# Sparse attention loop: eight score buffers, four score banks, one bank for the sums, and two heads' small probabilities in one copy

## The chip, the cores and the metric

The kernel runs on one core of a Trainium2 chip, in one launch. The metric is the device time of a run in microseconds (us), as the median of several runs; lower is better. PE is the TensorE (matmuls and transposes), DVE the VectorE, ACT the ScalarE, POOL the GpSimd engine, SP the SyncE. All numbers are float32.

## The reference, cut to what matters

Two decoder layers over 512 tokens of width 1024. Layer 0 is an mLSTM and differential attention with an FFN, layer 1 is native sparse attention with an FFN. The change touches only one part of layer 1: the two of its three attention branches that are computed as masked dense attention (the gathered top-6 blocks, and the window of 256 keys), with 16 heads of 64 features in 4 key/value groups:

```python
s_s = jnp.einsum('bqghd,bgqmd->bghqm', qr, k_g).astype(jnp.float32) * scale
p_s = jax.nn.softmax(jnp.where(mask_s, s_s, NEG_INF), axis=-1)
o_s = jnp.einsum('bghqm,bgqmd->bqghd', p_s.astype(v_g.dtype), v_g)
```

and the same for the window with its keys. Both outputs are multiplied by a sigmoid gate of each token and head, and added to the output of the compressed branch.

## The kernel before, in words

The engines run separate instruction streams, written out by hand, and meet only by semaphores. In layer 1 the projections end, the compressed branch is computed, and then comes **the loop** that the change is in. Behind it the summed rows are turned back to features (L1066, L1435, L2061) and the output projection begins (L551 to L553).

The loop's unit of work is a *set* `n`: one block of 128 queries, one branch, one head. There are 128 sets: four query blocks, two branches, sixteen heads. `SET_ORDER` (L171) puts them in this order of query block and branch, each for all sixteen heads: sets 0 to 47 have three key tiles of 128 keys, sets 48 to 63 four, sets 64 to 95 two, sets 96 to 127 one. Eight sets of one kind are a *batch* `b`, 16 in all. What is done for a set:

- *scores* (`set_scores`, L1000, PE): one matmul, 64 features deep, 128 queries by 128 to 512 keys, into bank `n % 2` of the PSUM tensor `aux`.
- *max* (`set_max`, L2013, DVE): one instruction scales, adds the mask, writes the negated scores to the score buffer `sr[n % 4]` and gives the row's negated maximum.
- *exp* (L1419, ACT): the exponential in place in the same buffer, with the row's sum.
- *turn* (`set_turn`, L1009, PE): one transpose per key tile, into bank `2 + n % 2` of `aux`.
- *take* (`take_probs`, L475 on ACT, L477 on DVE): the turned probabilities copied to SBUF, every third set by ACT, the others by DVE.

And for a batch:

- *values* (`set_values`, L1023, PE): one pair of matmuls for each key tile, 512 columns each, one key tile per step; the sums of the batch add up in a PSUM bank called `OB`.
- the sums copied by ACT (L1431, `branch_sums`, which frees `OB`), turned by PE (`sums_turn`, L1033) into a bank called `OT`, multiplied with the coefficients (the reciprocal sum times the gate, L2021 and L2025) by DVE (`batch_out`, L2036, which frees `OT`), and added to the output rows by POOL (L2222). `OB` and `OT` have two banks each, used in turns (L155).

All engines go through the loop in *steps* `n = 0, 2, 4, ...`, two sets at a time. A step of PE is: scores of sets `n` and `n+1`; turns of sets `n-4` and `n-3`; `sums_turn` if a batch has its turn; then at most one key tile of values for a batch. Values of batch `b` begin at step `8b + 12`. A step of DVE: two maxes; one of the 16 instructions of the top-6 selection and its masks (`select_step`, one each in steps 2 to 32); its takes of `n-4`, `n-3`; coefficients; `batch_out`. A step of ACT: two exps; its takes; the copy of sums.

The waits that order the loop before the change: the scores of step `n` wait until both maxes of step `n-2` are done (L995), since there are two score banks. The max of set `n` waits until set `n-4` is turned (L2003), since there are four score buffers, and that turn stands in PE's stream behind the scores of the same step. The turn of set `n` waits for the take of set `n-2` (L1007), since there are two turn banks. Everything that an engine's stream has behind a waiting instruction waits too.

The banks before: `aux` 0 and 1 scores, `aux` 2 and 3 turns, the four banks of `abank` for `OB` and `OT`. No weight is loaded during the loop; the output projection's first weights are already split when it begins.

Of the kernel before, what the change touches and what calls it, by code (L numbers as in the profile page):

```python
# [11 lines left out]
P = 128  # L12
D = 1024
T = 512
# [202 lines left out]
def on_act(n):  # L217

    return n % 3 == 0


def taken_before(n):

    return sum(on_act(k) == on_act(n) for k in range(n + 1))
# [11 lines left out]
def trunk(nc, A, consts, out):  # L236
    with ExitStack() as ctx:
# [95 lines left out]
        sr = [row(f"score{s}", 36 + s if s < 3 else 6, 1) for s in range(4)]  # L333
# [17 lines left out]

        TR = abank[2][:, 0:P]
# [112 lines left out]
        def take_probs(eng, n):  # L465

            i, win, h = set_of(n)
            w = set_tiles(i, win) * P
            eng.wait_ge(S("s_turned"), n + 1)
            b = n // 8  # L470
            if b >= 2:
                eng.wait_ge(S("s_sum"), b - 1)
            dst = eT[b % 2][:, n % 8 * T:n % 8 * T + w]
            if on_act(n):
                eng.activation(dst, aux[:, 2 + n % 2, 0:w], ACT.Copy).then_inc(S("probs_by_act"), 1)  # L475
            else:
                eng.tensor_copy(dst, aux[:, 2 + n % 2, 0:w]).then_inc(S("probs_by_dve"), 1)  # L477

        def wait_probs(eng, n):
            eng.wait_ge(S("probs_by_act" if on_act(n) else "probs_by_dve"), taken_before(n))  # L480
# [67 lines left out]
        def _(pe):  # L548
# [453 lines left out]

            def set_turn(n):
                i, win, h = set_of(n)
                pe.wait_ge(S("s_exp"), n + 1)
                if n >= 2:
                    wait_probs(pe, n - 2)  # L1007
                for s in range(set_tiles(i, win)):
                    mm = pe.transpose(aux[:, 2 + n % 2, col(s)], sr[n % 4][:, col(s)], ident)  # L1009
                mm.then_inc(S("s_turned"), 1)  # L1010

            def set_values(b, s):
                i, win, h = set_of(8 * b)
                keys, tiles = set_keys(i, win), set_tiles(i, win)
                if s == 0:
                    wait_probs(pe, 8 * b + 7)
                    wait_probs(pe, 8 * b + 6)
                    wait_probs(pe, 8 * b + 5)
# [19 lines left out]
            for n in range(0, sums_turned_at(NSETS // 8 - 1) + 4, 2):  # L1038
# [10 lines left out]
                for b in batches_at(sums_turned_at, n - 2):  # L1049
# [6 lines left out]
            for q in range(8):  # L1056
# [4 lines left out]
                else:  # L1061
                    wait_probs(pe, NSETS - 1)
                    wait_probs(pe, NSETS - 2)
# [12 lines left out]
        def _(act):  # L1076
# [333 lines left out]
            for n in range(0, sums_turned_at(NSETS // 8 - 1) + 2, 2):  # L1410
                for m in (n, n + 1):
                    if m >= NSETS:
                        break
# [5 lines left out]
                    act.activation(sr[m % 4][:, 0:w], sr[m % 4][:, 0:w], ACT.Exp, scale=-1.0,  # L1419
                                   bias=nmx[:, m % 16:m % 16 + 1], accum_out=rsum[:, m % 16:m % 16 + 1])\  # L1420
                       .then_inc(S("s_exp"), 1)
                for m in (n - 4, n - 3):
                    if 0 <= m < NSETS and on_act(m):
                        if m == 0:
                            act.wait_ge(S("c_sum"), 2 * TT)
                        take_probs(act, m)
                for b in batches_at(sums_turned_at, n):
                    if b >= 2:
                        act.wait_ge(S("sums_turned"), b - 1)
                    act.wait_ge(S("s_sum"), b + 1)  # L1430
                    act.activation(osum[b % 2], ps(("OB", b))[:, :], ACT.Copy).then_inc(bank_free(("OB", b)), 1)  # L1431
# [29 lines left out]
        def _(dve):  # L1461
# [537 lines left out]
            def set_max(n):  # L1999
                i, win, h = set_of(n)  # L2000
                w = set_tiles(i, win) * P
                if n >= 4:
                    dve.wait_ge(S("s_turned"), n - 3)  # L2003
# [9 lines left out]
                dve.tensor_tensor_reduce(sr[n % 4][:, 0:w], aux[:, n % 2, 0:w], mask, -(HD ** -0.5), BIG,  # L2013
                                         ALU.add, ALU.min, nmx[:, n % 16:n % 16 + 1]).then_inc(S("s_max"), 1)

            def batch_coef(b):
# [6 lines left out]
                if b >= 2:  # L2023
                    wait_taken(dve, ("OT", b - 2))
# [17 lines left out]
            for n in range(0, sums_turned_at(NSETS // 8 - 1) + 4, 2):  # L2042
# [8 lines left out]
                for m in (n - 4, n - 3):  # L2051
                    if 0 <= m < NSETS and not on_act(m):
                        take_probs(dve, m)
# [205 lines left out]
```

## Time and profile before

| what | us |
|---|---|
| median of three runs | 1431.55 |
| the three runs | 1424.27, 1431.55, 1432.41 |
| the profiled execution, whole | 1428.94 |
| its span, first to last instruction | 1427.1 |
| the loop within it, first scores to last turned sums | 823.0 to about 992 |
| PE busy in the span | 1355.2 (95%) |
| DVE, ACT, POOL busy in the span | 711.1, 551.5, 279.2 |

The profile is of one execution, and the times inside it add up to its own span; around the span lie 1.84 us. The median of the other runs is 2.6 us above that execution. "Busy" counts an instruction from its first to its last moment; matmuls overlap one another at their ends, so that PE is shown busy where it only drains. Where a text speaks of the *spacing* of instructions, it means from start to start, which has no such overlap.

### The profile page before, as it was taken

Reading aid. Unit: us, or ns where it says so; the run is one execution under the profiler, and the core shown is the slowest. Engines: PE = TensorE matmul, PEld = TensorE weight load, DVE = VectorE, ACT = ScalarE, POOL = GpSimd, SP = SyncE. Lnnn points to the kernel's source line nnn. Section 1 sums busy time; section 2 is a strip of 40 time slices with the busy share of each in tenths; the row PEclk is TensorE's granted clock in tenths of the full one; section 3 lists DMA queues with packets and bytes.
Section 4 is the critical chain, followed back from the end, with each engine's and each line's share of the span. In section 5 each row is a group of like instructions: output and inputs, shape, how many; then the busy total and the mean of one; then the engine's idle time right before and its main releaser. Section 6 shows DMA issues by size and latency. Waiting matters only on the chain.

```text
span 1427.1 us, 18120 instructions
## 1 busy us (share of the span) xinstructions
PE 1355.2 (95%) x6431; PEld 1059.5 (74%) x6431; DVE 711.1 (50%) x1279; ACT 551.5 (39%) x1009; POOL 279.2 (20%) x268
## 2 busy tenths in 40 slices
PE   7999989999999999999999988987989999999998
PEld 6777667888888888888777744444778888888887
DVE  4459865544434333333898677665344343433222
ACT  4335655433333322222453345565243333332222
POOL 2057352221111110011355001112111111111010
PEclk9999999999999999999999999998899999999999
DMA  7322221333333334322343200000123333343321
GB/s 219 89 59 60 59 60 45 89 89 103 88 103 90 101 108 118 88 83 74 103 118 107 62 16 1 1 1 1 59 74 103 103 88 103 89 119 101 101 61 60
DMA packets 203946, 114.12 MB, mean 80 GB/s; under 512 B 5713, under 2 KB 200529, under 8 KB 203761
## 3 DMA queue, kind: packets, MB, share of 16 engines
q1 hardware_dynamic: 203264, 112.97, 27.0%
q0 software_dynamic: 416, 0.35, 0.3%
q8 instruction: 33, 0.54, 0.2%
q14 instruction: 25, 0.20, 0.0%
q10 hardware_dynamic: 208, 0.06, 0.0%
HBM read 111.27 MB, written 2.10 MB: 79 GB/s over the span
## 4 chain that ended last, share of the span: by engine, by line
PE 81%; DVE 8%; ACT 5%; issue 3%; POOL 2%; DMA 0%; DVEq 0%; POOLq 0%; SPq 0%; ACTq 0%
PE acc L551 23%; PE acc L553 22%; PE acc L552 22%; PE aux L1009 3%; PE aux L1000 2%; PE acc L1023 2%; DVE w_low L459 2%; ACT score L1419 1%; ACT w_high L440 1%; DVE cmp_in_low L1685 1%; PE acc L1033 1%; PE acc L960 0%; PE aux L678 0%; PE aux L668 0%; DVE work L1532 0%
## 5 line engine op out<-in xcount | busy, mean ns | idle before, releaser
L459 DVE TENSOR_TENSOR w_low<-raw,w_high 128x1024 fp32r<-128x1024 f32 (+1 forms) x187 | 250.7, 1341 | 531.5 <-ACT w_high L440 531.2
L551 PE MATMUL acc<-y_high,w_high 128*128 128x512 f32 x1056 | 421.2, 399 | 12.0 <-DVE w_low L451 6.4
L552 PE MATMUL acc<-y_low,w_high 128*128 128x512 f32 x1056 | 414.8, 393 | 0.0
L553 PE MATMUL acc<-y_high,w_low 128*128 128x512 f32 x1056 | 414.7, 393 | 0.0
L440 ACT ACTIVATE w_high<-raw 128x1024 fp32r<-128x1024 f32 (+1 forms) x187 | 206.8, 1106 | 345.1 <-PE acc L553 336.1
L551 PEld LDWEIGHTS acc<-y_high,w_high 128*128 128x128 f32 x1056 | 200.2, 190 | 57.5 <-DVE w_low L451 7.9
L553 PEld LDWEIGHTS acc<-y_high,w_low 128*128 128x128 f32 x1056 | 199.9, 189 | 43.2
L552 PEld LDWEIGHTS acc<-y_low,w_high 128*128 128x128 f32 x1056 | 200.3, 190 | 41.8 <-issue 0.7
L551 PE MATMUL acc<-ffn_high,w_high 128*128 128x512 f32 (+1 forms) x374 | 141.0, 377 | 0.0
L552 PE MATMUL acc<-ffn_low,w_high 128*128 128x512 f32 (+1 forms) x374 | 140.8, 377 | 0.0
L553 PE MATMUL acc<-ffn_high,w_low 128*128 128x512 f32 (+1 forms) x374 | 140.8, 377 | 0.0
L2139 POOL TENSOR_TENSOR work<-work,work 128x512 f32<-128x512 f32 x44 | 57.0, 1295 | 417.6 <-DVE work L1488 417.6
L1419 ACT ACTIVATE score<-score,neg_max 128x384 f32<-128x384 f32 (+3 forms) x128 | 69.1, 541 | 64.7 <-DVE neg_max L2013 64.6
L2125 POOL TENSOR_TENSOR work<-work,work 128x512 f32<-128x512 f32 x31 | 41.8, 1347 | 228.1 <-ACT work L1086 227.7
L1488 DVE TENSOR_TENSOR work<-acc,rinv 128x512 f32<-128x512 f32 x107 | 73.2, 684 | 24.6 <-PE acc L553 17.1
L1267 ACT ACTIVATE ffn_high<-work 128x512 f32 (+1 forms) x44 | 27.8, 633 | 148.5 <-POOL work L2139 148.5
L551 PEld LDWEIGHTS acc<-ffn_high,w_high 128*128 128x128 f32 x374 | 70.4, 188 | 13.0
L553 PEld LDWEIGHTS acc<-ffn_high,w_low 128*128 128x128 f32 x374 | 70.4, 188 | 12.8
L552 PEld LDWEIGHTS acc<-ffn_low,w_high 128*128 128x128 f32 x374 | 70.4, 188 | 12.8
L2013 DVE CUSTOM_DVE_ANT_0 score<-aux,shape_constants 128x384 f32<-128x384 f32 (+2 forms) x112 | 45.8, 441 | 40.4 <-PE aux L1009 39.4
L1009 PEld LDWEIGHTS aux<-shape_constants,score 128*128 128x128 f32 x304 | 32.6, 140 | 35.8 <-ACT score L1419 29.9
L1262 ACT ACTIVATE work<-work 128x512 f32<-128x512 f32 x44 | 27.8, 633 | 80.3 <-DVE work L1488 80.3
(282 smaller groups left out, 1597.5 us busy)
## 6 DMA issues: line engine op xcount, KB each, us to landing
raw<-in_l_w_in_dram SPq DMA_DIRECT2D x44, 512.0 KB, 3.7
raw<-in_l_w_gate_dram SPq DMA_DIRECT2D x44, 512.0 KB, 3.7
raw<-in_l_w_up_dram SPq DMA_DIRECT2D x44, 512.0 KB, 3.7
raw<-in_l_w_down_dram SPq DMA_DIRECT2D x32, 704.0 KB, 4.5
raw<-in_l_w_out_dram SPq DMA_DIRECT2D x16, 512.0 KB, 3.5
x_rows<-in_x_dram SPq DMA_DIRECT2D x4, 512.0 KB, 5.6
raw<-in_l_cmp_w_k_dram SPq DMA_DIRECT2D x4, 512.0 KB, 3.6
raw<-in_l_cmp_w_v_dram SPq DMA_DIRECT2D x4, 512.0 KB, 3.8
```

The source lines that it names most:

```text
L440: act.activation(dst, src, ACT.Copy).then_inc(S("split_high"), 1)
L459: dve.tensor_tensor(dst, src, high.bitcast(F32), ALU.subtract).then_inc(S("split_low"), 1)
L551: pe.matmul(o, ah, bh, start=first, stop=False)
L552: pe.matmul(o, ah, bl, start=False, stop=False)
L553: return pe.matmul(o, al, bh, start=False, stop=last)
L1000: pe.matmul(aux[:, n % 2, 0:keys.stop - keys.start], qrot[a, q], k, start=True, stop=True).then_inc(S("s_scores"), 1)
L1009: mm = pe.transpose(aux[:, 2 + n % 2, col(s)], sr[n % 4][:, col(s)], ident)
L1419: act.activation(sr[m % 4][:, 0:w], sr[m % 4][:, 0:w], ACT.Exp, scale=-1.0, bias=nmx[:, m % 16:m % 16 + 1], accum_out=rsum[:, m % 16:m % 1 ...
L1488: return dve.tensor_tensor(dst, ps(tile)[lo:hi, cols], rinv[lo:hi, cols], ALU.mult)
L2013: dve.tensor_tensor_reduce(sr[n % 4][:, 0:w], aux[:, n % 2, 0:w], mask, -(HD ** -0.5), BIG, ALU.add, ALU.min, nmx[:, n % 16:n % 16 + 1]).t ...
L2125: pool.tensor_tensor(tmp[0][:, 0:T], tmp[0][:, 0:T], tmp[1 + m % 2][:, 0:T], ALU.add)\
L2139: pool.tensor_tensor(up, tmp[2 * (t % 2)][:, 0:T], up, ALU.mult).then_inc(S("ffn_prod"), 1)
```

## The change

It rewrites who may use which buffer in the loop, and the order of a few steps; each matmul, transpose, max and exponential stays.

1. Score buffers: eight instead of four (`sr`), in rows of SBUF that are free by then. The max of set `n` waits for the turn of set `n-8`.
2. Score banks: four instead of two (`SCORE`): `aux` 0 and 1, `abank` 2 and 3. The scores of step `n` wait for the maxes of step `n-4`. The scores of sets 2 and 3, whose banks held the compressed branch's last tiles, wait until those were read (`OC` 6 and 7).
3. Sums: `OB` has only bank 0, `OT` only bank 1. `sums_turn` comes one step earlier in PE's stream (in the step in which ACT copies the sums), and ACT's copy stands before the step's exps instead of after its takes.
4. Takes: sets of one or two key tiles are turned two at a time into one bank (the second set behind the first), and copied by one instruction of twice the width; that is sets 64 to 127. Of all takes, counted one after another, every third is ACT's. Turn banks of these pairs alternate by pair.
5. The wait for `OT` in `batch_coef` stands before the reciprocal.

```diff
         elif kind in ("OB", "OT"):
-            b = k % 2 + 2 * (kind == "OT")
+            b = int(kind == "OT")
...
-def on_act(n):
-
-    return n % 3 == 0
...
+TAKES = []
+for _n in range(0, NSETS, 2):
+    TAKES += [(_n, 2)] if set_tiles(*set_of(_n)[0:2]) <= 2 else [(_n, 1), (_n + 1, 1)]
+TAKE_OF = {first + k: t for t, (first, count) in enumerate(TAKES) for k in range(count)}
...
+def on_act(t):
+
+    return t % 3 == 0
...
+def turn_bank(n):
+
+    return 2 + (n // 2 if TAKES[TAKE_OF[n]][1] == 2 else n) % 2
...
+def turn_column(n):
+
+    return n % 2 * set_tiles(*set_of(n)[0:2]) * P if TAKES[TAKE_OF[n]][1] == 2 else 0
...
+def taken_first(n):
+
+    return [max(TAKE_OF[m] for m in range(n) if turn_bank(m) == turn_bank(n) and TAKE_OF[m] < TAKE_OF[n])] if n >= 2 else []
...
-        sr = [row(f"score{s}", 36 + s if s < 3 else 6, 1) for s in range(4)]
+        sr = [row(f"score{s}", r, 1) for s, r in enumerate((36, 37, 38, 6, 41, 7, 42, 43))]
...
+        SCORE = [aux[:, 0, :], aux[:, 1, :], abank[2][:, :], abank[3][:, :]]
...
-            dst = eT[b % 2][:, n % 8 * T:n % 8 * T + w]
-            if on_act(n):
-                eng.activation(dst, aux[:, 2 + n % 2, 0:w], ACT.Copy).then_inc(S("probs_by_act"), 1)
+            dst = eT[b % 2].rearrange("p (h t) -> p h t", t=T)[:, n % 8:n % 8 + count, 0:w]
+            src = aux[:, turn_bank(n), 0:count * w].rearrange("p (h t) -> p h t", h=count)
+            if on_act(t):
+                eng.activation(dst, src, ACT.Copy).then_inc(S("probs_by_act"), 1)
...
-                if n >= 2:
-                    pe.wait_ge(S("s_max"), n // 2 * 2)
+                if n >= 4:
+                    pe.wait_ge(S("s_max"), n // 2 * 2 - 2)
+                elif n >= 2:
+                    for k in (6, 7):
+                        wait_taken(pe, ("OC", k))
...
-                pe.matmul(aux[:, n % 2, 0:keys.stop - keys.start], qrot[a, q], k,
+                pe.matmul(SCORE[n % 4][:, 0:keys.stop - keys.start], qrot[a, q], k,
...
-                if n >= 2:
-                    wait_probs(pe, n - 2)
+                for t in taken_first(n):
+                    wait_probs(pe, t)
+                c = turn_column(n)
                 for s in range(set_tiles(i, win)):
-                    mm = pe.transpose(aux[:, 2 + n % 2, col(s)], sr[n % 4][:, col(s)], ident)
+                    mm = pe.transpose(aux[:, turn_bank(n), c + s * P:c + (s + 1) * P], sr[n % 8][:, col(s)], ident)
...
-                for b in batches_at(sums_turned_at, n - 2):
+                for b in batches_at(sums_turned_at, n):
                     sums_turn(b)
...
+                for b in batches_at(sums_turned_at, n):
+                    if b >= 2:
+                        act.wait_ge(S("sums_turned"), b - 1)
+                    act.wait_ge(S("s_sum"), b + 1)
+                    act.activation(osum[b % 2], ps(("OB", b))[:, :], ACT.Copy).then_inc(bank_free(("OB", b)), 1)
+                for m in range(n, min(n + 2, NSETS)):
...
-                if n >= 4:
-                    dve.wait_ge(S("s_turned"), n - 3)
+                if n >= 8:
+                    dve.wait_ge(S("s_turned"), n - 7)
...
                 dve.wait_ge(S("s_exp"), 8 * b + 8)
+                if b >= 2:
+                    wait_taken(dve, ("OT", b - 2))
                 dve.reciprocal(coef[:, c:c + 8], rsum[:, c:c + 8]).then_inc(S("s_recip"), 1)
                 dve.wait_ge(S("s_recip"), b + 1)
-                if b >= 2:
-                    wait_taken(dve, ("OT", b - 2))
```

## Rows read from the trace of the kernel before

**Rows 1.** The page: the chain that ended last, share of the span by engine.

```profile
PE 81%; DVE 8%; ACT 5%; issue 3%; POOL 2%; DMA 0%; DVEq 0%; POOLq 0%; SPq 0%; ACTq 0%
```

**Rows 2.** Windows of the loop's five stretches: us, busy us (instructions) of PE, PEld, DVE, ACT, POOL, then the granted clock.

```profile
830.93:841.51 10.58, 7.06 (x41) 3.74 (x41) 7.40 (x26) 5.98 (x19) 0.00 (x0) 1.00 0.00 0
841.51:893.80 52.29, 46.98 (x253) 21.26 (x253) 38.32 (x123) 30.07 (x91) 5.10 (x4) 1.00 0.00 1
893.80:919.90 26.10, 23.54 (x126) 10.88 (x125) 17.59 (x49) 15.57 (x41) 2.54 (x2) 1.00 0.01 1
919.90:957.89 37.99, 35.27 (x202) 16.47 (x201) 24.90 (x99) 23.07 (x81) 5.09 (x4) 1.00 0.01 1
957.89:986.11 28.22, 22.36 (x138) 11.73 (x136) 17.17 (x97) 18.16 (x80) 5.08 (x4) 1.00 0.00 1
```

**Rows 3.** Source view of L1000 (scores): what ended PE's idle time before it, us and times.

```profile
  DVE neg_max L2013: 63.2, 80
```

**Rows 4.** Timeline, a step without values: start us, us, engine, line, operation, idle before.

```profile
836.45 0.92 PE L1000 MATMUL aux<-k_win_dup,q_rot 64*128 64x384 f32 x4 [0.81 <-DVE neg_max L2013]
...
837.30 1.00 PE L1009 MATMUL aux<-shape_constants,score 128*128 128x128 f32 x6
...
837.88 0.56 DVE L2013 CUSTOM_DVE_ANT_0 score<-aux,shape_constants 128x384 f32<-128x384 f32 x1 [0.90 <-PE aux L1009]
...
838.98 0.92 PE L1000 MATMUL aux<-k_win_dup,q_rot 64*128 64x384 f32 x4 [0.68 <-DVE neg_max L2013]
```

**Rows 5.** Timeline of PE, a step of three tiles with values, and the next scores.

```profile
844.62 0.92 PE L1000 MATMUL aux<-k_win_dup,q_rot 64*128 64x384 f32 x4
...
845.47 0.88 PE L1009 MATMUL aux<-shape_constants,score 128*128 128x128 f32 x6
...
846.27 1.08 PE L1023 MATMUL acc<-probs_T,v_sel_win 128*64 128x512 f32 x4
...
847.28 0.92 PE L1000 MATMUL aux<-k_win_dup,q_rot 64*128 64x384 f32 x4
```

**Rows 6.** Timeline of PE, the sums turned and the values after them.

```profile
854.51 0.66 PE L1033 MATMUL acc<-shape_constants,branch_sums 128*128 128x128 f32 x4
...
855.10 1.08 PE L1023 MATMUL acc<-probs_T,v_sel_win 128*64 128x512 f32 x4
```

**Rows 7.** Timeline of DVE ahead of the loop's second step.

```profile
828.20 1.49 DVE L1991 TENSOR_TENSOR o_rows<-acc,gates 128x512 f32<-128x512 f32 x2 [1.24 <-PE acc L960]
```

**Rows 8.** Timeline of PE, a step of four tiles.

```profile
906.59 1.13 PE L1000 MATMUL aux<-k_sel_dup,q_rot 64*128 64x512 f32 x4
...
907.65 1.09 PE L1009 MATMUL aux<-shape_constants,score 128*128 128x128 f32 x8
...
908.67 1.08 PE L1023 MATMUL acc<-probs_T,v_sel_win 128*64 128x512 f32 x4
```

**Rows 9.** Timeline of PE, a step of two tiles.

```profile
930.45 0.70 PE L1000 MATMUL aux<-k_win_dup,q_rot 64*128 64x256 f32 x4
...
931.08 0.66 PE L1009 MATMUL aux<-shape_constants,score 128*128 128x128 f32 x4
...
931.67 1.08 PE L1023 MATMUL acc<-probs_T,v_sel_win 128*64 128x512 f32 x4
```

**Rows 10.** Timeline of PE, one tile: scores and turns.

```profile
971.03 0.49 PE L1000 MATMUL aux<-k_win_dup,q_rot 64*128 64x128 f32 x4
...
971.46 0.44 PE L1009 MATMUL aux<-shape_constants,score 128*128 128x128 f32 x2
```

**Rows 11.** Timeline of DVE: a copy of 512 columns, and two of 256.

```profile
925.00 0.69 DVE L477 COPY probs_T<-aux 128x512 f32<-128x512 f32 x1
...
927.36 0.75 DVE L477 COPY probs_T<-aux 128x256 f32<-128x256 f32 x2
```

**Rows 12.** Windows where the loop drains and behind it; columns as in rows 2.

```profile
988.00:990.00 2.00, 1.24 (x5) 0.20 (x4) 1.92 (x4) 0.27 (x1) 1.27 (x1) 0.80 0.00 0
...
991.95:1003.27 11.32, 7.95 (x35) 6.03 (x34) 6.23 (x9) 4.79 (x8) 1.26 (x1) 0.50 0.01 1
```

More of the change, by code:

```diff
@@ L214, in batches_at, with taken_before @@
     return [b for b in range(NSETS // 8) if at(b) == n]
-def on_act(n):
-    return n % 3 == 0
-def taken_before(n):
-    return sum(on_act(k) == on_act(n) for k in range(n + 1))
+TAKES = []
[4 more added lines that the diff above has]
+    return t % 3 == 0
+def taken_before(t):
+    return sum(on_act(k) == on_act(t) for k in range(t + 1))
+def turn_bank(n):
[4 more added lines that the diff above has]
+    return [max(TAKE_OF[m] for m in range(n) if turn_bank(m) == turn_bank(n) and TAKE_OF[m] < TAKE_OF[n])] if n >= 2 else []
 def gain_at(n, m, it=0):
@@ L463, in cmp_view, with take_probs @@
             return kvd[v].rearrange("p (g t) -> p g t", t=T)[:, :, 2 * c:2 * c + 16 * (NCMP - 1) + 1:16]
[L465 to L469, printed above, removed]
+        def take_probs(eng, t):
+            n, count = TAKES[t]
+            w = set_tiles(*set_of(n)[0:2]) * P
+            eng.wait_ge(S("s_turned"), n + count)
             b = n // 8
@@ L472, in take_probs, with wait_probs @@
                 eng.wait_ge(S("s_sum"), b - 1)
[L473 to L480 removed]
+            dst = eT[b % 2].rearrange("p (h t) -> p h t", t=T)[:, n % 8:n % 8 + count, 0:w]
+            src = aux[:, turn_bank(n), 0:count * w].rearrange("p (h t) -> p h t", h=count)
+            if on_act(t):
+                eng.activation(dst, src, ACT.Copy).then_inc(S("probs_by_act"), 1)
+            else:
+                eng.tensor_copy(dst, src).then_inc(S("probs_by_dve"), 1)
+        def wait_probs(eng, t):
+            eng.wait_ge(S("probs_by_act" if on_act(t) else "probs_by_dve"), taken_before(t))
         block = ctx.enter_context(nc.Block())
@@ L1015, in set_values @@
                 if s == 0:
-                    wait_probs(pe, 8 * b + 7)
-                    wait_probs(pe, 8 * b + 6)
-                    wait_probs(pe, 8 * b + 5)
+                    for t in range(TAKE_OF[8 * b + 7] - 2, TAKE_OF[8 * b + 7] + 1):
+                        wait_probs(pe, t)
                     wait_bank(pe, ("OB", b))
@@ L1037, in _ @@
             pe.wait_ge(S("rope_done"), 60)
-            for n in range(0, sums_turned_at(NSETS // 8 - 1) + 4, 2):
+            for n in range(0, sums_turned_at(NSETS // 8 - 1) + 2, 2):
                 if n < NSETS:
@@ L1061, in _ @@
                 else:
-                    wait_probs(pe, NSETS - 1)
-                    wait_probs(pe, NSETS - 2)
+                    wait_probs(pe, len(TAKES) - 1)
+                    wait_probs(pe, len(TAKES) - 2)
                 for m in range(4):
@@ L1418, in _ @@
                         act.wait_ge(S("s_coef"), m // 8 - 1)
-                    act.activation(sr[m % 4][:, 0:w], sr[m % 4][:, 0:w], ACT.Exp, scale=-1.0,
+                    act.activation(sr[m % 8][:, 0:w], sr[m % 8][:, 0:w], ACT.Exp, scale=-1.0,
                                    bias=nmx[:, m % 16:m % 16 + 1], accum_out=rsum[:, m % 16:m % 16 + 1])\
                        .then_inc(S("s_exp"), 1)
-                for m in (n - 4, n - 3):
-                    if 0 <= m < NSETS and on_act(m):
-                        if m == 0:
+                for t, (first, _count) in enumerate(TAKES):
+                    if first in (n - 4, n - 3) and on_act(t):
+                        if t == 0:
                             act.wait_ge(S("c_sum"), 2 * TT)
-                        take_probs(act, m)
-                for b in batches_at(sums_turned_at, n):
-                    if b >= 2:
-                        act.wait_ge(S("sums_turned"), b - 1)
-                    act.wait_ge(S("s_sum"), b + 1)
-                    act.activation(osum[b % 2], ps(("OB", b))[:, :], ACT.Copy).then_inc(bank_free(("OB", b)), 1)
+                        take_probs(act, t)
             for q in range(8):
@@ L2050, in _ @@
                     select_step(n // 2 - 1)
-                for m in (n - 4, n - 3):
-                    if 0 <= m < NSETS and not on_act(m):
-                        take_probs(dve, m)
+                for t, (first, _count) in enumerate(TAKES):
+                    if first in (n - 4, n - 3) and not on_act(t):
+                        take_probs(dve, t)
                 if n >= 10 and n % 8 == 2 and n < NSETS + 10:
```

6 lines of the change are left out of this document (1 added, 5 removed).

## The prediction

> **What bounds the kernel now.** I read the page's chain first [rows 1]: 81% of the span is on PE, almost all in the big projections, which the change leaves alone. So the question is one stretch of 170 us. I cut it where the kind of scores changes, at the first scores of steps 4, 12, 48, 64 and 96, up to the end of step 126, and read the windows of the five parts [rows 2]: A (steps 4 to 10, no values yet) 10.58 us, B (12 to 46, three tiles) 52.29, C (48 to 62, four tiles) 26.10, D (64 to 94, two tiles) 37.99, E (96 to 126, one tile) 28.22; in all 155.2 us for 62 steps. In none is an engine full: PE shows 135.2 us busy with overlaps counted twice, DVE 95.4, ACT 92.9. Three engines short of full, and the source view of the scores names what PE waits for: DVE's max, 63.2 us over 80 records [rows 3] (weight loads and matmuls are counted apart, so about half of it is wall time). That is the two-bank ring.
>
> The timeline shows the ring turning [rows 4]. Scores start at 836.45, the turns at 837.30, the first max only at 837.88, because it waits for the turn of set `n-4`, 1.43 us after the scores began. Two maxes take 1.10 us to 838.98, where the next scores start at once. The step lasts 2.53 us, although PE issues only 0.85 + 0.80 us of work in it. Where values fill the gap, it is the other way round [rows 5]: 844.62 to 847.28 is 2.66 us, put together without a hole from scores 0.85, turns 0.80, values 1.01. There PE is the bound already, and nothing can be gained in such a step. The gain lies in the steps with little PE work, and in the unevenness between steps.
>
> **Step by step: the floor of PE.** Spacings from the rows: two scores cost 0.85 us (three tiles) [rows 5], 1.06 (four) [rows 8], 0.63 (two) [rows 9], 0.43 (one) [rows 10]; turns of two sets 0.80, 1.02, 0.59 and, of one tile, at most 0.44 with their end, at least the half of that without it: I take 0.35; 0.45 for two tiles where no values follow, between 0.35 and 0.59. A key tile of values is 1.01 (V), sums turned 0.59 (U) [rows 5, 6]. The number of V and U in each part follows from `values_at` and the new place of `sums_turn`:
>
> A: 4 x (0.85 + 0.80) = 6.6. B: 18 x 1.65, 14 V, 4 U: 29.7 + 14.1 + 2.4 = 46.2. C: 8 x 1.06, turns 2 x 0.80 + 6 x 1.02, 6 V, 2 U: 8.5 + 7.7 + 6.1 + 1.2 = 23.5. D: 16 x 0.63, turns 2 x 1.02 + 10 x 0.59 + 4 x 0.45, 12 V, 4 U: 10.1 + 9.7 + 12.1 + 2.4 = 34.3. E: 16 x 0.43, turns 2 x 0.45 + 14 x 0.35, 5 V, 5 U: 6.9 + 5.8 + 5.1 + 3.0 = 20.8. Together 131.4, against 155.2: at most 23.8 us can go.
>
> **What the other engines leave of it, part by part.** Four score banks and eight buffers (edits 1 and 2) remove both links of the ring: scores need the maxes of two steps back, and the max no longer waits for a turn. What is late next is the turn's wait for the take of the step before. For three tiles, counted from the scores' start: 0.6 to the first result, 1.1 for two maxes [rows 4], about 0.4 for a selection step, two takes of about 0.5 each (between 0.75 for two of 256 columns and 0.69 for one of 512 [rows 11]): 3.1. The next turns come one step plus 0.85 later, so this binds only steps under 2.25 us. V steps (2.66) and U steps (2.24) clear it; the steps of A (1.65) don't.
> - A: DVE's own work is 7.40/4 = 1.85 per step [rows 2]; with the wait above about 2.1. I take 8.4, gain 2.2; bounds 6.6 and 10.58. In it is a late start: scores of step 2 now wait for DVE's last reads of the compressed branch, which end at 828.20 + 1.49 = 829.69 [rows 7]. The max of that step followed these reads on DVE anyway, and now comes at most 0.6 later; the next steps catch up, as scores may run ahead.
> - B: DVE 38.32/18 = 2.13 per step, PE's mean 2.57. DVE's coefficients and `batch_out` fall into the two steps behind a U step and put a max back by half a microsecond once a batch. I add 1.0 to 46.2: 47.2, gain 5.1; bounds 46.2 and 50.5.
> - C: DVE 2.20, ACT 1.95 per step against PE's 2.94: 23.7, gain 2.4.
> - D: DVE 1.56, ACT 1.44 against 2.14. A pair of takes by one instruction costs 0.69 where two cost 0.75 [rows 11], and turn banks now last two steps instead of one, so no turn waits. 34.9, gain 3.1; bounds 34.3 and 37.
> - E: the three engines lie close: PE 1.30 per step, ACT 18.16/16 = 1.14, DVE 1.07. In-order engines so near each other can't all be full; V and U steps (1.79, 1.37) alternate with steps of 0.78, in which ACT's 1.14 counts. Two steps of 1.14, one of 1.79 and one of 1.37 are 5.4 a batch, four of them 21.8; with DVE's coefficients and sums in the short steps I take 23.8, gain 4.4; bounds 20.8 and 27.
>
> Sum: 2.2 + 5.1 + 2.4 + 3.1 + 4.4 = 17.2 us.
>
> Edit 3 (one bank for the sums) I cost at nothing. `OB` must be copied by ACT (about 0.6 for 512 columns, a bank of the size of the 0.69 of DVE's copy [rows 11]) before the next batch's first V; between the last V and that one lie scores and turns of at least one step, 2.08 for four tiles [rows 8], where the next V follows closest. ACT's copy is queued ahead of two exps, but the first of these waits for a max that ends 1.1 after the scores' start. `OT` has eight sets' time to be read. `sums_turn` a step earlier falls, for three tiles, into the step that has no values, which evens PE out. If this cover were gone, the price is in the third rival. Edit 5 moves a wait on DVE's own earlier work: nothing. The tail behind step 126, and the row turns with their two engines behind them (11.32 us [rows 12]), stay. SP's and POOL's streams are untouched; no weight moves in the loop.
>
> A rule that speaks against edit 3: the Trainium skill, "Perfetto Trace Analysis", section "Optimizing Tensor Performance", says that independent groups of matmuls should rotate through different PSUM banks, so that the evacuation of one lies beside the next one's matmuls. The change takes this rotation from the sums and gives it to the scores. By the rule the sums' copy would be exposed; by the trace other matmuls fill that time, and the sum above stands. No run here shows it yet.
>
> The profiled execution would become 1428.94 - 17.2 = 1411.7. The median lies 2.6 above it; splitting this, I say 1413.0.
>
> **The rivals.**
> 1. Near the floor: gain 22 to 27. For it: B, C and D are PE-bound by my own numbers, and the clock falls to half (0.50 of 2.4, which is 1.2 GHz) only where the loop drains [rows 12]; a denser E might hold it. If the 11.32 us behind the loop ran at full clock, PE's 7.95 would halve, of which at most 3 are on its path. Against: E. Time 1428.94 - 24 + 1 = 1406.
> 2. The takes replace the ring: two turn banks remain, and if DVE reaches its takes some 0.3 us later than I have it, each step of A, B and C pays that, 30 x 0.3 = 9. Gain 8, time 1421 to 1423. For it: DVE shows 2.13 busy in a 2.9 us step already. Against: 0.4 us of room in the V steps.
> 3. Slower: the single `OB` bank, with ACT's copy ahead of the exps. By my count ACT ends a step's take about 2.9 after the scores' start, 0.25 after the end of a V (2.66), and then copies until 0.9 after it; the next exps could begin at 1.1. If ACT comes over 0.5 behind the V instead, copy and exps queue up, PE's `sums_turn` and the first V of the next batch wait for the copy, and the turns for the exps: copy 0.6 and two exps 1.3 (ACT's 1.67 per step [rows 2] less its takes), 1.9 on the path, once a batch, 16 x 1.9 = 30, less the 17 gained. Time about 1442. Against: scores and turns lie between the V and `sums_turn`, and two steps between an exp and its turn.
> 4. The limits are elsewhere and nothing moves: gain under 4, about 1430. Against: rows 4 show the wait itself.
>
> **How the numbers follow.** Forecast 0.56 (gain 12 to 22, or 1407 to 1419), rival 1 0.12, rival 2 0.22, rival 3 0.04, rival 4 0.06. The range reaches over the forecast into rivals 1 and 2: 1404 to 1423. A change of 1%, 14.3 us, is what a measurement of this kernel can tell from none. Faster by more than that, under 1417.2: all of rival 1 and most of the forecast, 0.12 + 0.56 less a part at its slow end, plus a little of rival 2's fast end, and the 2.6 us between profile and median mostly on my side: 0.70. Within 1%: 0.26. Slower: 0.04.
>
> **What would show it.** Right: a step without values lasts 1.7 to 2.2 us; PE's idle time before scores falls from 63.2 to under 10, and what is left moves to the turns, released by ACT's exps or the takes; V steps of three tiles stay at 2.66; A to E together last about 138; the takes of sets 64 to 127 are 32 instructions where they were 64. Wrong: PE idle ahead of the values or of L1033 with ACT's `branch_sums` as releaser (rival 3), or turns that wait for L477 in most steps of B (rival 2), or a granted clock below 1.00 inside the loop.

## The result, and the profile after

The changed kernel takes 1413.36 us (median of four runs, 1411.44 to 1416.21), the kernel before, with a fourth run beside it, 1428.32. The ratio is 0.9886, with a 95% interval of 0.9858 to 0.9914: 1.1% faster. Forecast were 1413.0 us. The span of the profiled execution fell from 1427.1 to 1411.6 us, by 15.5.

The page of the changed kernel, the chain by engine (as rows 1):

```profile
PE 83%; DVE 8%; ACT 4%; issue 3%; POOL 2%; DMA 0%; DVEq 0%; POOLq 0%; SPq 0%; ACTq 0%
```

81% have become 83%: more of the last chain lies on PE. The windows of the same five stretches (as rows 2: us, busy us of PE, PEld, DVE, ACT, POOL, then the granted clock), cut again at the first scores of steps 4, 12, 48, 64 and 96, then the row turns behind the loop:

```profile
831.10:841.33 10.23, 8.25 (x43) 4.48 (x39) 7.93 (x27) 5.87 (x18) 0.00 (x0) 0.83 0.00 0
841.33:889.64 48.31, 46.27 (x254) 21.36 (x253) 39.17 (x125) 31.06 (x91) 5.10 (x4) 1.00 0.00 1
889.64:913.54 23.90, 23.23 (x127) 10.88 (x125) 17.75 (x48) 15.65 (x41) 2.53 (x2) 1.00 0.01 1
913.54:948.84 35.30, 34.51 (x203) 16.56 (x201) 23.97 (x90) 22.64 (x76) 5.10 (x4) 1.00 0.00 1
948.84:973.19 24.35, 21.61 (x142) 11.82 (x141) 15.84 (x86) 17.78 (x75) 5.07 (x4) 1.00 0.00 1
...
977.75:987.68 9.93, 5.88 (x34) 4.23 (x34) 6.22 (x9) 4.78 (x8) 1.26 (x1) 0.84 0.01 2
```

PE's work is the same and now fills the windows: in C it is busy 23.23 of 23.90 us, before 23.54 of 26.10 [rows 2]. The gains are 0.35 in A, 3.98 in B, 2.20 in C, 2.69 in D and 3.87 in E, 13.1 in all. The first scores came 0.55 later in this execution and the first two steps lasted 0.38 less; the drain (986.11 to 991.95 before, 973.19 to 977.75 now) gave 1.3, and the row turns 1.4, with about two thirds of that stretch at full clock this time (mean 0.84, before 0.50 [rows 12]). Together that is the 15.5.

What ended PE's idle time in the changed kernel, before the scores (source view of L1026, first line) and before the turns (source view of L1036, the other two); us, times:

```profile
  DVE neg_max L2037: 23.7, 33
```

```profile
  ACT score L1448: 22.0, 29
...
  ACT probs_T L498: 4.8, 8
```

The wait for the max fell from 63.2 [rows 3] to 23.7 us. In the last line stand ACT's takes. They are few microseconds, but A shows what they do. Its second step, `n = 6`, takes 3.67 us (832.77 to 836.44). The timeline of the changed kernel in that step:

```profile
832.77 0.92 PE L1026 MATMUL acc<-k_win_dup,q_rot 64*128 64x384 f32 x4
...
833.71 0.56 DVE L2037 CUSTOM_DVE_ANT_0 score<-aux,shape_constants 128x384 f32<-128x384 f32 x1
833.84 0.61 ACT L1448 ACTIVATE score<-score,neg_max 128x384 f32<-128x384 f32 x1 [0.63 <-DVE neg_max L2037]
...
834.45 0.60 ACT L1448 ACTIVATE score<-score,neg_max 128x384 f32<-128x384 f32 x1
...
835.05 0.47 ACT L498 ACTIVATE probs_T<-aux 128x384 f32<-128x384 f32 x1
...
835.66 0.84 PE L1036 MATMUL aux<-shape_constants,score 128*128 128x128 f32 x6 [1.98 <-ACT probs_T L498]
```

Set 0 was turned by 832.4, but its take stands in ACT's stream behind the exps of sets 4 and 5, and these wait for late maxes. So it begins at 835.05, and PE stands still for 1.98 us with a turn that wants the bank. 1.3 us after that pause the clock is at its lower level, 1.2 GHz, from 837.0 to 840.4 (window of the changed kernel, columns as above; 0.57 is the mean of full and half):

```profile
837.00:841.00 4.00, 4.00 (x18) 2.13 (x15) 2.36 (x8) 1.40 (x5) 0.00 (x0) 0.57 0.00 0
```

### The profile page after: what moved, and what is told of

Same layout as the page of the kernel before. It is cut to its first block, busy times and chain, and to the rows that moved or that the text cites. A ratio compares the mean times of both kernels' runs of the same rounds, so it can differ in the third digit from the quotient of the medians.

```text
span 1411.6 us, 18054 instructions
## 1 busy us (share of the span) xinstructions
PE 1352.6 (96%) x6431; PEld 1060.6 (75%) x6431; DVE 708.7 (50%) x1258; ACT 550.5 (39%) x998; POOL 277.9 (20%) x268
## 4 chain that ended last, share of the span: by engine, by line
PE 83%; DVE 8%; ACT 4%; issue 3%; POOL 2%; DMA 0%; DVEq 0%; POOLq 0%; SPq 0%; ACTq 0%
PE acc L574 23%; PE acc L575 23%; PE acc L576 23%; PE acc L1049 3%; PE aux L1036 2%; DVE w_low L481 1%; PE acc L1026 1%; PE aux L1026 1%; ACT w_high L462 1%; DVE cmp_in_low L1709 1%; ACT score L1448 1%; PE aux L961 1%; PE acc L1059 1%; PE acc L983 0%; PE acc L659 0%
## 5 line engine op out<-in xcount | busy, mean ns | idle before, releaser
L575 PE MATMUL acc<-ffn_low,w_high 128*128 128x512 f32 (+1 forms) x374 | 140.9, 377 | 0.0
L576 PE MATMUL acc<-ffn_high,w_low 128*128 128x512 f32 (+1 forms) x374 | 140.9, 377 | 0.0
L1036 PEld LDWEIGHTS aux<-shape_constants,score 128*128 128x128 f32 x304 | 32.7, 142 | 32.3 <-ACT score L1448 22.0
L2246 POOL TENSOR_TENSOR o_rows<-o_rows,work 128x512 f32<-128x512 f32 x16 | 20.3, 1270 | 179.6 <-DVE work L2060 179.6
```

What stands on the lines that cost most here:

```text
L575: pe.matmul(o, ah, bl, start=False, stop=False)
L576: return pe.matmul(o, al, bh, start=False, stop=last)
L1036: mm = pe.transpose(aux[:, turn_bank(n), c + s * P:c + (s + 1) * P], sr[n % 8][:, col(s)], ident)
```

## The experiments

Beside each time stands the ratio to the kernel before with its interval; medians of before were 1428.5 to 1430.3 in these sessions. "Loop" is first scores to first row turn, from the start of their matmuls: 169.16 us before, 154.41 changed. A to E are the stretches as above; E ends with the first turn of step 128, which in the kernel before begins at 986.14. Each row of stretches is one execution. In A the clock was at half for a time in the changed kernel and e4, in E in e2, e3 and f3; all other entries of A to E are at full clock. So a second measure stands in the text where it matters: from the first scores to the scores of step 116, before the clock fell in E in any of them.

| kernel | A | B | C | D | E | loop | median | ratio |
|---|---|---|---|---|---|---|---|---|
| before | 10.58 | 52.29 | 26.10 | 37.99 | 28.25 | 169.16 | | |
| changed | 10.23 | 48.31 | 23.90 | 35.30 | 24.35 | 154.41 | 1413.36 | 0.9886 |
| e1, buffers alone | 8.45 | 49.37 | 24.90 | 36.33 | 26.22 | 158.23 | 1418.79 | 0.9934 |
| e2, banks and sums alone | 10.28 | 51.58 | 24.99 | 38.06 | 31.91 | 169.02 | 1427.36 | 0.9993 |
| e3, sums alone | 10.57 | 50.84 | 25.69 | 38.15 | 30.45 | 169.68 | 1430.42 | 0.9996 |
| e4, no pairs | 10.21 | 48.30 | 23.90 | 35.89 | 25.69 | 156.45 | 1415.37 | 0.9899 |
| f1, early banks | 9.06 | 48.22 | 23.89 | 35.31 | 24.37 | 151.84 | 1411.38 | 0.9871 |
| f2, ACT takes first | 8.14 | 46.52 | 23.15 | 34.76 | 23.61 | 148.08 | 1408.23 | 0.9848 |
| f3, coefficients later | 9.06 | 48.39 | 23.69 | 35.31 | 25.24 | 153.65 | 1410.96 | 0.9876 |
| f4, f1 to f3 and more | 7.85 | 45.58 | 23.15 | 34.77 | 22.46 | 144.79 | 1404.79 | 0.9818 |
| g1, e1 and takes first | 8.41 | 48.66 | 24.48 | 35.67 | 25.31 | 156.38 | 1414.26 | 0.9890 |
| g2, e2 and takes first | 7.27 | 48.10 | 24.17 | 35.92 | 25.55 | 153.72 | 1416.19 | 0.9913 |
| g3, f4 without f3 | 7.86 | 45.59 | 23.14 | 34.77 | 23.62 | 147.13 | 1407.97 | 0.9854 |
| h1, f4, DVE takes first | 7.27 | 47.86 | 24.18 | 36.10 | 24.00 | 150.39 | 1407.78 | 0.9868 |

### Which link of the ring: buffers or banks

e1 is the kernel before with eight buffers:

```diff
-                if n >= 4:
-                    dve.wait_ge(S("s_turned"), n - 3)
+                if n >= 8:
+                    dve.wait_ge(S("s_turned"), n - 7)
```

and `sr` with eight rows, used by `n % 8`.

> The kernel before with eight score buffers and nothing else: the max no longer waits for a turn, the scores still wait for both maxes of the step before. Theory (the ring of 2.53 us is made of two links, and one of them is enough to open it): scores 0.6 + two maxes 1.1 is a ring of 1.7 us, shorter than a step with values, so that steps without values fall from 2.5 to about 2.0 and the loop (168.95 us before, first scores to first row turn) to about 160; time 8 to 10 us below before. Rival (the two score banks are the bound): nearly nothing, loop above 166.

e2 is the changed kernel without its buffers and pairs:

```diff
-    TAKES += [(_n, 2)] if set_tiles(*set_of(_n)[0:2]) <= 2 else [(_n, 1), (_n + 1, 1)]
+    TAKES += [(_n, 1), (_n + 1, 1)]
...
-                if n >= 8:
-                    dve.wait_ge(S("s_turned"), n - 7)
+                if n >= 4:
+                    dve.wait_ge(S("s_turned"), n - 3)
```

and `sr` with four rows, used by `n % 4`.

> The changed kernel with four score buffers as before and no pairs: only the banks (four for scores, one each for sums) and the order of the sums are new. Theory (one link is enough): PE may issue scores ahead, the max still starts behind a turn, loop about 159 to 161, 8 to 10 us below before. Rival (buffers are the link that counts): loop above 165.

Measured: the buffers alone give 10.9 us of loop and 0.9934 (0.9912 to 0.9955); the banks alone give nothing that the time shows, 0.9993 (0.9979 to 1.0007). So my theory that either link opens the ring fell, and the rival that the buffers count stands. The loop of e2, 169.02 us, is hurt by the clock in its last steps (its window, columns as above):

```profile
972.70:986.30 13.60, 13.18 (x48) 6.75 (x48) 5.91 (x36) 7.29 (x31) 1.27 (x1) 0.50 0.00 0
```

From the first scores to those of step 116 the kernel before takes 152.6 us, e1 143.3 and e2 150.0. So at full clock e2 does gain 2.6 us, where e1 gains 9.3. Of the 2.6, e3 below, which has no new score bank, shows 1.4. The windows of e1, its first stretch, against rows 2:

```profile
830.81:839.26 8.45, 6.92 (x40) 3.73 (x40) 7.40 (x26) 5.97 (x19) 0.00 (x0) 1.00 0.00 0
```

The same instructions on every engine as in the kernel before, but for a record of PE, and 2.1 us shorter. Why the banks don't help is in the timeline of e2:

```profile
855.83 0.49 PE L1036 MATMUL aux<-shape_constants,score 128*128 128x128 f32 x3
856.09 0.55 DVE L2037 CUSTOM_DVE_ANT_0 score<-acc,shape_constants 128x384 f32<-128x384 f32 x1
...
856.68 0.61 ACT L1448 ACTIVATE score<-score,neg_max 128x384 f32<-128x384 f32 x1 [1.51 <-DVE neg_max L2037]
...
857.29 0.60 ACT L1448 ACTIVATE score<-score,neg_max 128x384 f32<-128x384 f32 x1
...
857.89 0.47 ACT L498 ACTIVATE probs_T<-aux 128x384 f32<-128x384 f32 x1
858.50 0.84 PE L1036 MATMUL aux<-shape_constants,score 128*128 128x128 f32 x6 [0.33 <-ACT probs_T L498]
859.06 0.56 DVE L2037 CUSTOM_DVE_ANT_0 score<-aux,shape_constants 128x384 f32<-128x384 f32 x1 [1.14 <-PE aux L1036]
```

A second ring runs through the same wait: max 856.09, two exps, take 857.89, turn 858.50, and only then the next max at 859.06, which needs that turn for its buffer: 2.97 us, through three engines, and no score bank is in it. It is in the kernel before too. There step 6 lasts 2.98 us (833.47 to 836.45). From one first max to the next, through ACT's take and the turn that waits for it, it is 2.98 us as well:

```profile
832.37 0.56 DVE L2013 CUSTOM_DVE_ANT_0 score<-aux,shape_constants 128x384 f32<-128x384 f32 x1 [0.53 <-PE aux L1009]
...
834.18 0.47 ACT L475 ACTIVATE probs_T<-aux 128x384 f32<-128x384 f32 x1
834.79 0.85 PE L1009 MATMUL aux<-shape_constants,score 128*128 128x128 f32 x6 [0.41 <-ACT probs_T L475]
835.35 0.56 DVE L2013 CUSTOM_DVE_ANT_0 score<-aux,shape_constants 128x384 f32<-128x384 f32 x1 [1.31 <-PE aux L1009]
```

If this ring holds e2, early takes must open it. g2 is e2 with the takes ahead of ACT's exps and of DVE's maxes. On DVE:

```diff
+                for t, (first, _count) in enumerate(TAKES):
+                    if first in (n - 4, n - 3) and not on_act(t):
+                        take_probs(dve, t)
                 if n < NSETS:
                     set_max(n)
                     set_max(n + 1)
...
-                for t, (first, _count) in enumerate(TAKES):
-                    if first in (n - 4, n - 3) and not on_act(t):
-                        take_probs(dve, t)
```

> The kernel with four score banks and four buffers (loop 169.02 us, no gain) with the takes ahead of ACT's exps and ahead of DVE's maxes. Theory (banks alone gave nothing because a second ring of the same length remains: max waits for a turn, the turn for a take, the take stands behind this step's maxes and exps; 0.6 + 1.2 + 0.5 + 0.6 = about 2.9 us): with takes first that ring is cut to turn, take, next turn, and the loop falls to 155 to 160. Rival (four buffers bound it by the exps, whatever the takes do): loop above 165.

The loop fell from 169.02 to 153.72 us, further than expected, 0.9913 (0.9895 to 0.9930), with four buffers still. A part of that is e2's half clock; up to step 116 it is 150.0 to 138.2 us, 11.8 less. The second ring is shown. Which of the two moves, ACT's or DVE's, did how much of it was not separated here.

### The sums' single bank

e3 is the kernel before with edits 3 and 5 only, as in the diff of the change: ACT's copy of the sums moves ahead of the exps, and

```diff
-            b = k % 2 + 2 * (kind == "OT")
+            b = int(kind == "OT")
...
-                for b in batches_at(sums_turned_at, n - 2):
+                for b in batches_at(sums_turned_at, n):
                     sums_turn(b)
```

> The kernel before with one bank each for OB and OT, sums turned a step earlier and ACT's copy ahead of the exps; nothing else. Theory (handing the bank over is hidden): same as before within 1.5 us, perhaps 1 faster as the sums fall into a step without values. Rival (exposed handover, 1.9 us a batch): loop 16 x 1.9 = 30 us longer; or 0.6 a batch, 10 us longer.

0.9996 (0.9978 to 1.0015): nothing, as expected. B and C lose 1.9 us (sums now fall into a step without values), E reads 2.2 longer, but in that execution the clock went to half inside E, so its end can't be compared. The handover costs nothing here.

### The pairs

e4 is the changed kernel with single takes throughout:

```diff
-    TAKES += [(_n, 2)] if set_tiles(*set_of(_n)[0:2]) <= 2 else [(_n, 1), (_n + 1, 1)]
+    TAKES += [(_n, 1), (_n + 1, 1)]
```

> The changed kernel without pairs: each set of two or one tiles is turned into its own bank and copied by its own instruction. Theory: only the sets from 64 on differ; a pair copy saves 0.06 us of DVE and a turn bank lasts a step longer, so the two-tile stretch (35.30 us) is at most 0.5 longer and the one-tile stretch (24.35) 1 to 3 longer: 1 to 3 us above the changed kernel. Rival (the pairs carry the gain of those stretches): both go back towards 38.0 and 28.2, 6 us above the changed kernel.

A, B and C stay, D is 0.59 (a little over the 0.5 expected) and E 1.34 us longer, 2.0 in the loop, as expected. The total, 0.9899 (0.9874 to 0.9925), doesn't tell it from the changed kernel. The loops of e1 (buffers), e4 (buffers, banks, sums) and the changed kernel (and pairs) go 158.23, 156.45, 154.41; the latter two hold the half clock in A, which is priced next.

### What holds the changed kernel: the first steps and the takes

f1 puts the scores' extra banks where DVE is done sooner:

```diff
-            b = int(kind == "OT")
+            b = 2 + int(kind == "OT")
...
-        SCORE = [aux[:, 0, :], aux[:, 1, :], abank[2][:, :], abank[3][:, :]]
+        SCORE = [aux[:, 0, :], aux[:, 1, :], abank[0][:, :], abank[1][:, :]]
...
-                    for k in (6, 7):
+                    for k in (4, 5):
```

> The changed kernel with the score banks 2 and 3 laid where the compressed branch is read earlier (abank 0 and 1; OB and OT take abank 2 and 3; the wait is for OC 4 and 5). Theory (the late start of the second scores costs the first steps their gain): the scores of step 2 start with no wait for DVE, first scores to step 12 falls from 17.78 us to about 16.8, the loop from 154.41 to about 153.4. Rival (that start is hidden): no change within 0.3 us.

Two steps ahead of A shrank from 7.55 to 6.64 us, as expected. A fell by 1.17 too, and here no half clock came; f3, whose code in A is that of the changed kernel, shows the same 9.06 at full clock (its window in A):

```profile
828.92:837.98 9.06, 6.84 (x43) 3.75 (x39) 7.92 (x27) 5.96 (x19) 0.00 (x0) 1.00 0.00 0
```

So 0.9 us are the banks' and 1.17 is the clock's in the changed kernel's profile.

f2 moves the loop over `TAKES` in ACT's stream from behind the exps to ahead of them:

```diff
+                for t, (first, _count) in enumerate(TAKES):
+                    if first in (n - 4, n - 3) and on_act(t):
+                        if t == 0:
+                            act.wait_ge(S("c_sum"), 2 * TT)
+                        take_probs(act, t)
                 for m in range(n, min(n + 2, NSETS)):
```

> The changed kernel with ACT's takes ahead of its two exps. Theory (the 3.67 us step at n = 6 is a turn that waits for set 0's take, which stands behind two exps on ACT): this step falls to about 2.4, and with it goes PE's pause of 1.98 us, so that no half clock follows in steps 8 to 10; first scores to step 12 falls from 17.78 to about 15.5; steady steps unchanged; loop 151 to 152.5. Rival (what is late there is DVE's take): the step loses under 0.4 us. Second rival: exps come later everywhere, and the one-tile part gets longer by 1 to 3 us.

The 3.67 us step fell to 2.73, and more came than expected: the loop 6.3 us shorter than in the changed kernel, 1.8 of it in B, 0.75 in C, 0.5 in D, 0.7 in E. Of the rest, A has 0.9 against f3's 9.06 at full clock. The other 1.6 us are mostly the half clock that the changed kernel's profile had in A and in the drain. So 4.7 us in A to E are the edit's. The timeline of f2 at the same place:

```profile
830.80 0.88 PE L1036 MATMUL aux<-shape_constants,score 128*128 128x128 f32 x6
...
831.95 0.47 ACT L498 ACTIVATE probs_T<-aux 128x384 f32<-128x384 f32 x1
...
832.56 0.52 PE L1036 MATMUL aux<-shape_constants,score 128*128 128x128 f32 x3
...
833.89 0.52 PE L1036 MATMUL aux<-shape_constants,score 128*128 128x128 f32 x3 [0.81 <-DVE probs_T L500]
```

ACT's take now begins 1.15 us after the turns did, the next turn isn't held by it, and the second turn waits 0.81 for DVE's take instead. g1 asks whether the banks are worth anything then: it is e1 with the same move on ACT.

```diff
+                for m in (n - 4, n - 3):
+                    if 0 <= m < NSETS and on_act(m):
+                        if m == 0:
+                            act.wait_ge(S("c_sum"), 2 * TT)
+                        take_probs(act, m)
                 for m in (n, n + 1):
```

> The kernel before (its two score banks, two banks each for OB and OT, no pairs) with eight score buffers and ACT's takes ahead of its exps: what the four score banks, the sums' single banks and the pairs are worth once the ring is open and the takes are early. The eight buffers alone gave a loop of 158.23 us, taking first gave the changed kernel 6.3 more. Theory (banks and pairs add only in the uneven short steps): loop 151 to 154, that is 3 to 6 us above the 148.08 of the changed kernel with takes first. Rival (once the takes are early, two score banks are the bound): loop above 156.

Its loop is 156.38 us, 8.3 more than f2's; the expectation was 3 to 6, and the rival's bound was 156. Part of the 8.3 is the clock: g1's drain ran at half clock from 976.2 on. In A to E, with full clock in both, it is 142.5 against 136.2 us, 6.3 more, just above what I had expected; so the rival's bound, passed with half clock in the loop, doesn't decide for it. Without early takes, e1 against the changed kernel with f3's A, it is 145.3 against 140.9, 4.4 more. So with early takes the banks, the sums' place and the pairs are together worth more than without them.

### The coefficients beside POOL, and all together

f3 is the changed kernel with

```diff
-                if n >= 10 and n % 8 == 2 and n < NSETS + 10:
-                    batch_coef(n // 8 - 1)
+                if n >= 12 and n % 8 == 4:
+                    batch_coef((n - 12) // 8)
```

> The changed kernel with the coefficients computed one step later (step 8b + 12 for batch b), away from POOL's addition of the batch before. In the changed kernel the coefficient multiply (L2049) lasts 0.17 us in 13 of 16 batches, and 0.81, 0.48 and 0.89 in those in which POOL's L2246 runs. Theory (DVE is held by POOL, and this reaches PE in the one-tile part): all 16 near 0.17, one-tile part 0.5 to 1.5 us shorter (24.35 before the edit). Rival (hidden): durations fall, the part stays within 0.3.

The edit didn't do what I meant: the longest of the 16 multiplies is still 0.83 us, as POOL's additions are met one step later as well. E was 0.9 us longer, with half clock in it from 961.8 to 965.2. f4 joins the three edits and puts DVE's takes ahead of the selection step:

```diff
+                for t, (first, _count) in enumerate(TAKES):
+                    if first in (n - 4, n - 3) and not on_act(t):
+                        take_probs(dve, t)
                 if n == 0:
                     cmp_out(2)
                     cmp_out(3)
```

g3 is f4 with the coefficients back at `n % 8 == 2`.

> The three edits together, and DVE's takes ahead of its selection step. Theory (they act on different steps): first scores to step 12 about 15.0, three-tile part 47.0 to 48.0, loop about 149.5 to 151, time 3 to 5 us under the changed kernel. Rival: what one of them frees the next engine takes, loop above 152.

> The fastest version so far (loop 144.79 us) with the coefficients back at their old step. Theory (moving the coefficients did nothing of itself: beside POOL's additions they were as long as before): loop within 0.7 us of 144.79. Rival (they were on the path of the one-tile part, 22.46 us): that part 1 us or more longer.

The windows of f4, stretches A to E:

```profile
830.04:837.89 7.85, 6.84 (x43) 3.61 (x39) 7.70 (x28) 6.16 (x19) 0.00 (x0) 1.00 0.00 1
837.89:883.47 45.58, 45.58 (x253) 21.41 (x252) 38.61 (x125) 31.24 (x92) 5.10 (x4) 1.00 0.00 1
883.47:906.62 23.15, 23.15 (x126) 10.87 (x124) 17.91 (x49) 15.46 (x40) 2.57 (x3) 1.00 0.01 1
906.62:941.39 34.77, 34.60 (x202) 16.52 (x201) 24.31 (x90) 22.80 (x76) 5.11 (x4) 1.00 0.00 1
941.39:963.85 22.46, 21.46 (x142) 11.76 (x141) 15.63 (x86) 17.64 (x74) 5.09 (x4) 1.00 0.01 1
```

In B and C the busy time of PE is the window itself: nothing is left there but PE's own work. f4 is the fastest version: 1404.79 us, 0.9818 (0.9802 to 0.9835), and its loop of 144.79 us is well under the 149.5 to 151 expected. Against g3 all stretches agree but E, which is 1.16 us longer in g3, at full clock in both. So the rival's expectation for g3 held: the place of the coefficients does matter once the rest is open. The traces, one execution of each, show where. Nearly all of it is in two steps, 110 (1.92 us in g3, 1.57 in f4) and 118 (2.31 and 1.70). In step 118 PE waits for ACT's copy of the sums. These lines are g3's:

```profile
954.86 0.81 DVE L2049 TENSOR_TENSOR coef<-coef,gates 128x8 f32<-128x8 f32 x1
...
956.70 0.57 ACT L1441 ACTIVATE branch_sums<-acc 128x512 f32<-128x512 f32 x1
...
957.33 0.66 PE L1059 MATMUL acc<-shape_constants,branch_sums 128*128 128x128 f32 x4 [0.87 <-ACT branch_sums L1441]
```

and this one f4's:

```profile
958.19 0.65 PE L1059 MATMUL acc<-shape_constants,branch_sums 128*128 128x128 f32 x4 [0.26 <-ACT branch_sums L1441]
```

In g3 the reciprocal and a multiply of 0.81 us stand ahead of the maxes of step 116 (955.60 and 955.81). Two exps wait for these, and the copy stands behind the exps. In f4 both maxes begin at 956.10 and 956.31, right behind those of step 114, and the multiply comes after them (957.09, 0.17 us). So the order of DVE's stream, with the long multiply in it, accounts for this step; the multiply's length alone, which was my reason for f3, was not tested by itself, and f3 alone showed no gain. Step 110 was not followed up.

h1 goes on from f4: DVE's takes move ahead of its maxes too, with the diff of g2.

> The fastest version so far (loop 144.79 us, median 1404.79) with DVE's takes ahead of its maxes, not only ahead of its selection step. Theory (takes are late only in the first steps now, a DVE take waits for a turn that PE issues after the scores, and a max behind it starts later): first steps up to 0.6 us shorter, the rest unchanged or up to 1 us longer; loop 144.2 to 146, time the same within 0.1%. Rival (the earlier a take the better, as on ACT): loop under 144.

The loop, 150.39 us, is 5.6 longer than f4's, outside both what I expected (144.2 to 146) and the rival (under 144); A is 0.6 shorter as expected, B to E are 1.0 to 2.3 longer. A take that DVE reaches before its turn is done holds back two maxes that could have started. In h1 the scores of step 50 begin at 887.92, and their max only at 890.51, behind two takes for which DVE waited 1.10 us:

```profile
887.92 1.13 PE L1026 MATMUL acc<-k_sel_dup,q_rot 64*128 64x512 f32 x4
...
889.57 1.02 DVE L500 COPY probs_T<-aux 128x384 f32<-128x384 f32 x2 [1.10 <-PE aux L1036]
...
890.51 0.68 DVE L2037 CUSTOM_DVE_ANT_0 score<-acc,sel_mask 128x512 f32<-128x512 f32 x1
```

With eight buffers the takes belong behind the maxes on DVE and ahead of the exps on ACT. The likely reason is that ACT's exps become ready later than the turn and DVE's maxes sooner; no run tests it by itself.

## Why the prediction was right, and where not

- The floor of PE by spacings was right within 0.6 us in B to D. Forecast for B to E: 46.2, 23.5, 34.3 and 20.8 us as the least; f4 reached 45.58, 23.15, 34.77 and 22.46. In B and C it lay 0.6 and 0.35 too high. There the turns and sums' turns took 0.15 less per batch in their new place: 0.71 + 0.53 us (changed kernel, 851.11 to 852.35) where I had 0.80 + 0.59. In E even f4 stays 1.7 us above it.
- The stretches of the changed kernel were forecast as 8.4, 47.2, 23.7, 34.9, 23.8, and measured 10.23, 48.31, 23.90, 35.30, 24.35. The sum of gains was 17.2 forecast, 13.1 measured. The term that was mis-sized is A, 2.2 expected and 0.35 measured. Its step was "the next steps catch up, as scores may run ahead". Scores did, but the turns did not. I had counted the turn's wait for a take on DVE's stream alone, and set 0's take is ACT's and stood behind two exps: the step of 3.67 us. 1.17 of the miss is the half clock that followed PE's pause. B is 1.1 over, from the same cause, since f2 takes 1.8 from it.
- The other 2.4 us of the result came from where I had put nothing: drain 1.3 and row turns 1.4, less 0.2 at the start. I had the clock there as rival 1's point with 3 us at most. So that 1413.0 lies so near 1413.36 is partly luck: 4.1 us too much gain in A to E, against 2.4 that I had put nowhere and the 1.3 that I had added for the median.
- The reading of the ring was wrong in its main link. I wrote "That is the two-bank ring" because the scores' wait is released by the max. e1 and e2 show that the banks alone give nothing that the time shows, and the buffers alone 10.9 of the 14.75 us of loop. The rows had it: in rows 4 the max itself starts late, behind a turn, and I named that too, but gave the gain to both edits together, so the sum didn't depend on the error.
- Rival 2, the takes in place of the ring, was partly true, though it named DVE's takes; ACT's were late, and cost the changed kernel 4.7 us in A to E at full clock. That is about half of what parts it from the floor (A to E 140.9 us with f3's A, floor 131.4).
- Edit 3 at nothing was right (e3), and rival 3 did not happen: PE's idle time before the sums' turns, released by ACT's copy, is 5.1 us in 9 records against 5.0 in 9 before. The Trainium skill's rule on rotating banks ("Perfetto Trace Analysis", "Optimizing Tensor Performance") doesn't bind here, as other matmuls lie between the sums of two batches. For the scores too, four rotating banks gave next to nothing until buffers or takes were free (e2, g2).
- Pairs: 2.0 us of loop measured. Forecast "no turn waits" and 0.06 a pair.
- Of the signs I named, the scores' wait fell to 23.7, not under 10, and the clock did fall inside the loop once; A to E lasted 142.1 us and not 138. The idle time before the turns, released by exps or takes, did not grow but fell, from 36.0 to 26.8 us. Steps with values stayed at 2.66, and takes of sets 64 to 127 are 32.
- A slip in the working: DVE's busy time in the five stretches of rows 2 adds up to 105.4 us, not 95.4. The parts use the single numbers, so the sum is untouched.

## What to carry to other kernels

A wait that ends last names the releaser, not the resource: write down every ring of waits that closes over one step, with all its engines and its length, and ask which edits cut all rings that are longer than the busiest engine's step. Here freeing one resource (buffers) cut two rings and freeing another (banks) cut one of two and gave next to nothing. In an in-order stream put first what is ready first: moving copies ahead of exponentials on ACT, with no buffer more, took 4.7 us off A to E at full clock, about a third of what the whole change took off the loop, and the same move on DVE ahead of the maxes cost 5.6 us.

## What was not expected of the hardware

A pause of PE of 1.98 us in a stretch that is otherwise well filled was followed by half clock from 837.0 to 840.4, in code that at another time (f3, with a pause of 1.96 us at the same place) ran at full clock: 1.17 us for A. In e4 the half clock came there too, from 836.7. Where the clock first fell near the loop's end moved from 961.8 us (f3) to 990.6 us (e1), and in h1 it didn't fall; in e2, e3 and f3 that lay inside E, in others behind it. So a microsecond or two of the totals is not the edit's. The stretches at full clock are the better measure.

DVE's coefficient multiply, 128 x 8 elements with both inputs in SBUF, lasts 0.17 us, and up to 0.89 in the changed kernel when POOL adds 128 x 512 beside it. Two lines of the changed kernel's timeline:

```profile
963.95 1.26 POOL L2246 TENSOR_TENSOR o_rows<-o_rows,work 128x512 f32<-128x512 f32 x1 [3.32 <-DVE work L2060]
...
964.43 0.81 DVE L2049 TENSOR_TENSOR coef<-coef,gates 128x8 f32<-128x8 f32 x1
```

It ends at 965.24, POOL's at 965.21. The Trainium skill ("SBUF — State Buffer", section "Who interferes with whom") says that a VectorE instruction with two SBUF inputs and a GpSimd instruction that reads SBUF lock each other out as a whole, and that one with at most one SBUF input, outside its two-port modes, doesn't contend. By that rule, the trace agrees, as the copy out of PSUM that DVE begins at 953.63, beside POOL's addition from 953.38 on, lasts 0.42 us like others of its size. (The copy reads no SBUF.)
